# Two transformer blocks on one core: wide moving operands in both mixers, row-tiled index scores, a shorter bias and head

## The reference, cut to what matters

```python
h = rms_norm(x, norm_mix_g[l])
proj = h @ w_in[l]                       # q, k, v, xr, gr, sc_b, sc_c, sc_x, g_pre
...
s_own = s_own + rel_table[t5_bucket(dist)].transpose(2, 0, 1)      # the bias, by head
...
x = x + (g_a * y_a + g_b * y_b + g_c * y_c) @ w_out[l]
x = x + jnp.square(jax.nn.relu(rms_norm(x, norm_mlp_g[l]) @ w_mlp_up[l])) @ w_mlp_down[l]
x = rms_norm(x, final_g)
...
h = rmsnorm(x, g_mix) @ w_in             # z, xbc, dt, q, k, v, qi, ki, wi
s = jnp.einsum("bqhd,bsd->bqhs", qi_b, k_idx) * (IDX_HEAD_DIM ** -0.5)   # 16 index heads of 64
score = jnp.einsum("bqhs,bqh->bqs", jax.nn.relu(s), wi_b)
```

## Time and profile before

| | |
|---|---|
| median of three runs | 2725.01 us (2724.94 to 2727.85) |
| the profiled execution | 2726.56 us |
| its span | 2724.6 us |
| mean granted TensorE clock | 0.999 |
| PE busy | 2714.4 us (100%) |
| PE weight loads | 2360.8 us (87%) |
| DVE busy | 1668.2 us (61%) |
| ACT busy | 1279.5 us (47%) |
| L1676, L1677, L1678, the first mixer's units | 896 matmuls each |
| L1708, L1709, L1710, the second mixer's units | 592 matmuls each |
| L1691, L1692, the up projections | 2048 matmuls each |
| DMA | 509 MB, mean 187 GB/s |

### The profile page before, as it was taken

The page is one execution under the profiler, slowest core; times in us unless marked ns, Lnnn a source line. Parts: engine busy times, 40 slices in busy tenths (PEclk is TensorE's granted clock), DMA queues, the critical chain, the costliest instruction groups (busy, mean ns, idle before and its releaser), DMA issues.

```text
span 2724.6 us, 42567 instructions
## 1 busy us (share of the span) xinstructions
PE 2714.4 (100%) x15146; PEld 2360.8 (87%) x15146; DVE 1668.2 (61%) x2329; ACT 1279.5 (47%) x1721; POOL 23.2 (1%) x52
## 2 busy tenths in 40 slices
PE   9999999999999999999999999999999999999999
PEld 7999998888888888888888889999888888888887
DVE  5576766555555655655656566777776565565654
ACT  5455555444444544444434554455454344444443
POOL 0100000000000000000000000000000000000000
PEclk9999999999999999999999999999999999999999
DMA  7655555666665555555555555544455655555555
GB/s 276 199 171 176 181 174 185 201 198 197 204 210 188 180 190 193 185 193 189 189 193 185 186 185 163 171 149 155 154 178 187 195 190 186 192 186 193 189 188 170
DMA packets 140614, 509.01 MB, mean 187 GB/s; under 512 B 15975, under 2 KB 16231, under 8 KB 140232
## 3 DMA queue, kind: packets, MB, share of 16 engines
q1 hardware_dynamic: 135448, 492.28, 54.7%
q0 software_dynamic: 2736, 10.75, 1.2%
q10 hardware_dynamic: 2304, 4.20, 0.4%
HBM read 502.96 MB, written 4.19 MB: 186 GB/s over the span
## 4 chain that ended last, share of the span: by engine, by line
PE 98%; DVE 1%; ACT 1%; ACTq 0%; issue 0%
PE acc L1691 18%; PE acc L1692 9%; PE acc L1726 4%; PE acc L1728 4%; PE acc L1727 4%; PE pS L1726 4%; PE pT L1726 4%; PE pS L1727 4%; PE pS L1728 4%; PE pT L1728 4%; PE pT L1727 4%; PE acc L1676 4%; PE acc L1678 4%; PE acc L1677 4%; PE acc L1708 3%; PE acc L1710 3%
## 5 line engine op out<-in xcount | busy, mean ns | idle before, releaser
L989 DVE TENSOR_TENSOR wlo<-raw,whi 128x1024 fp32r<-128x1024 f32 x938 | 1147.6, 1224 | 845.5 <-ACT whi L530 843.5
L530 ACT ACTIVATE whi<-raw 128x1024 fp32r<-128x1024 f32 x938 | 992.4, 1059 | 1030.2 <-PE pT L1728 344.2
L1691 PE MATMUL acc<-a_w,whi 128*128 128x512 f32 x2048 | 724.6, 399 | 0.1
L1692 PE MATMUL acc<-a_w,wlo 128*128 128x256 f32 x2048 | 575.1, 281 | 0.0
L1691 PEld LDWEIGHTS acc<-a_w,whi 128*128 128x128 f32 x2048 | 384.8, 188 | 96.6 <-DVE a_w L1019 0.8
L1692 PEld LDWEIGHTS acc<-a_w,wlo 128*128 128x128 f32 x2048 | 386.9, 189 | 0.3
L1676 PE MATMUL acc<-a_w,whi 128*128 128x256 f32 x896 | 257.6, 287 | 0.0
L1678 PE MATMUL acc<-a_w,wlo 128*128 128x256 f32 x896 | 253.5, 283 | 0.0
L1677 PE MATMUL acc<-a_w,whi 128*128 128x256 f32 x896 | 253.5, 283 | 0.0
L1676 PEld LDWEIGHTS acc<-a_w,whi 128*128 128x128 f32 x896 | 171.8, 192 | 3.4 <-issue 3.0
L1708 PE MATMUL acc<-a_w,whi 128*128 128x256 f32 x592 | 173.9, 294 | 0.0
(11 more groups left out here) (406 smaller groups left out, 4215.7 us busy)
## 6 DMA issues: line engine op xcount, KB each, us to landing
raw<-stream SPq DMA_DIRECT2D x938, 512.0 KB, 3.3
gbias<-gateb POOLq DMA_DIRECT2D x12, 256.0 KB, 3.7
xF<-x ACTq DMA_DIRECT2D x8, 256.0 KB, 9.4
X<-x_rows POOLq DMA_DIRECT2D x1, 2048.0 KB, 9.0
bias_scratch<-brow POOLq DMA_DIRECT2D x8, 256.0 KB, 3.4
out<-X ACTq DMA_DIRECT2D x8, 256.0 KB, 4.6
bias<-bias_scratch POOLq DMA_DIRECT2D x8, 128.0 KB, 3.5
wg<-gates POOLq DMA_DIRECT2D x8, 128.0 KB, 3.4
```

The costliest lines, as they stand in the source:

```text
L530: A(whi[:, slot, :], raw[:, slot, :], ACT.Copy).then_inc(s.hi_done, 1)
L989: TT(wlo[:, slot, :], raw[:, slot, :], whi[:, slot, :].bitcast(F32), SUB).then_inc(s.lo_done, 1)
L1691: MM(ps, wh, wide[:, k0 + k, :], start=start and k == 0, stop=False, skip_group_check=True)
L1692: last = MM(ps[:, 0:T], wl, wide[:, k0 + k, 0:T], start=False, stop=not start and k == KC - 1, skip_group_check=True)
```

## The change

- First mixer: `chunk` goes; its units use `chunk_wide`. ACT copies the upper half of the bank to `half` (the renamed `sqacc`), DVE adds it to the lower half and then multiplies by `rB`.
- The last three steps of a head's attention (transposes, `attn_pt` and `attn_pv`, `attn_hi`, `attn_lo`) come one unit later, except for the last head.
- Second mixer: `half_unit` takes the same form. `unit_half` on ACT and `unit_sum` on DVE replace the copies from the bank; scaled units get a second DVE product (`unit_scaled`). The square of q reads `q_f` in SBUF and comes after the next `prep`. PE waits for `u_sum` alone.
- Index scores: 64 rows for each of the two heads, to two banks, instead of 128 rows against two diagonal blocks.
- Bias: one matmul with the table repeated 16 times for each head, one copy, eight DMAs that write the same rows.
- The first gates use the banks pV and pN instead of `acc`; the wait for the last evacuation moves to the first output product.
- Head: ACT issues two of the `xF` loads, SP the other six, two ahead of each of chunks 1 to 3.

```diff
@@ sync
             sp.dma_start(par, params).then_inc(s.par_landed, 16)
-            for c in range(NSLOT):
+            load(0, 0)
+            for c in range(1, NSLOT):
+                for k in (2 * c, 2 * c + 1):
+                    sp.dma_start(xF[:, 2 * k:2 * k + 2, :], x[:, 2 * k:2 * k + 2, :]).then_inc(x_landed[k], 16)
                 load(c, c)
@@ scalar
+                if j == (3 if t.base == 7 else 4):
+                    attn_pt(t)
                 if j == 3:
-                    attn_pt(t)
...
-                if j == 4:
+                if j == (4 if t.base == 7 else 5):
                     attn_hi(t, tile(br[0][0], t))
...
-            for k in range(8):
+            for k in range(2):
                 act.dma_start(xF[:, 2 * k:2 * k + 2, :], x[:, 2 * k:2 * k + 2, :]).then_inc(x_landed[k], 16)
...
                     prep(c)
+                    if i == 0 and j == 1:
+                        act.wait_ge(s.bias_ps, 1)
+                        A(brow, pO, ACT.Copy).then_inc(s.bias_copied, 1)
                     if i:
                         side1(j, At(i - 1))
+                    a = L1_UNITS * i + j
+                    act.wait_ge(s.mm_done, c.value(2))
+                    if a >= 2:
+                        act.wait_ge(s.l1_summed, a - 1)
+                    apart(act)
+                    A(half[:, a % 2, :], acc[a % 2][:, T:2 * T], ACT.Copy).then_inc(s.l1_copied, 1)
                     prep(c.plus(1))
...
+            def unit_half(u):
+
+                unit_done(unit_end(u))
+                if u == 0:
+                    act.wait_ge(s.t_evac, 2 * G_K + 2)
+                if u >= 2:
+                    act.wait_ge(s.u_sum, u - 1)
                 apart(act)
+                A(sq[:, u % 2, :], unit_bank(u)[:, T:2 * T], ACT.Copy).then_inc(s.u_half, 1)
...
                 attn_exp(At(8 + h))
+                unit_half(17 + 2 * h)
                 l2_prep(c + 1)
@@ vector
+            def evac(a, dst):
+
+                dve.wait_ge(s.l1_copied, a.value(1))
+                if a.least() > 0:
+                    dve.wait_ge(s.evacuated, a.value())
+                TT(t2, acc[a.mod(2)][:, 0:T], half[:, a.mod(2), :], ADD).then_inc(s.l1_summed, 1)
+                dve.wait_ge(s.l1_summed, a.value(1))
+                TT(dst, t2, rB, MUL).then_inc(s.evacuated, 1)
...
+            def unit_sum(u, dst):
+
+                dve.wait_ge(s.u_half, u + 1)
+                if u:
+                    dve.wait_ge(s.u_sum, u)
+                TT(dst, unit_bank(u)[:, 0:T], sq[:, u % 2, :], ADD).then_inc(s.u_sum, 1)
+
+            def unit_scaled(u, dst):
+
+                if u > 9:
+                    dve.wait_ge(s.evacuated, A_L2 + (u - 8) // 2 if u < 26 else A_L2 + u - 17)
+                unit_sum(u, usum)
+                dve.wait_ge(s.u_sum, u + 1)
+                TT(dst, usum, rB, MUL).then_inc(s.evacuated, 1)
@@ tensor
-                    MM(ps[:, 0:T], wh, hi, start=half == 0 and k == 0, stop=False)
-                    MM(ps[:, 0:T], wh, lo, start=False, stop=False)
-                    last = MM(ps[:, 0:T], wl, hi, start=False, stop=half == 1 and k == KC - 1)
+                    m = 8 * half + k
+                    MM(ps, wh, a_w[:, m, :], start=half == 0 and k == 0, stop=False, skip_group_check=True)
+                    last = MM(ps[:, 0:T], wl, a_w[:, m, 0:T], start=False, stop=half == 1 and k == KC - 1, skip_group_check=True)
...
-                if j == 2:
+                if j == (2 if t.base == 7 else 3):
                     attn_transpose(t)
...
-            def bias_rows(j):
-                for h in (2 * j, 2 * j + 1):
-                    if h >= 2:
-                        pe.wait_ge(s.bias_copied, h - 1)
-                    MM((pG if h % 2 else pO)[:, 0:512], tab[0:33, h:h + 1].to_broadcast([33, P]), oh[0:33, :],
-                       start=True, stop=True).then_inc(s.bias_ps, 1)
...
-                    chunk(c, a, a_w, 0, stop=False)
-                    chunk(c.plus(1), a, a_w, 8, start=False)
+                    chunk_wide(c, a, a_w, 0)
+                    chunk_wide(c.plus(1), a, a_w, 8, start=False)
...
-                    if i == 0 and j < 4:
-                        bias_rows(j)
+                        MM(pO, tab[0:33, :], oh[0:33, :], start=True, stop=True).then_inc(s.bias_ps, 1)
...
-                    banks = tbanks(i)
+                    banks = pair_first if side == 0 else tbanks(i)
...
-                q = qib[:, n % 3, :]
-                MM(pT[:, 0:T].rearrange("p (h k) -> p h k", h=2), q[:, 0:128],
-                   kibd.rearrange("p (h k) -> p h k", h=2)[:, :, 0:128], start=True, stop=True)
-                MM(pS[:, 0:2 * T], q[:, 128:256], kibd, start=True, stop=True).then_inc(s.idx_pe, 1)
+                rows = [slice(64 * e, 64 * e + 64) for e in range(2)]
+                for e, ps in enumerate((pT, pS)):
+                    r = rows[e]
+                    MM(ps[:, 0:128], qib[r, n % 3, 0:128], kibd[r, T * e:T * e + 128], start=True, stop=True)
+                for e, ps in enumerate((pT, pS)):
+                    r = rows[e]
+                    last = MM(ps[:, 128:384], qib[r, n % 3, 128:256], kibd[r, T * e:T * e + T], start=True, stop=True)
+                last.then_inc(s.idx_pe, 1)
```

More of the change, by code:

```diff
@@ L175, in __init__ @@
         self.up_copied = make("up_copied")
+        self.l1_copied = make("l1_copied")
+        self.l1_summed = make("l1_summed")
         self.setup_act = make("setup_act")
@@ L181, in __init__ @@
         self.bias_copied = make("bias_copied")
+        self.bias_out = make("bias_out")
         self.causal_landed = make("causal_landed")
@@ L208, in __init__ @@
         self.cleared = make("cleared")
-        self.unit_copied = make("unit_copied")
+        self.u_half = make("u_half")
+        self.u_sum = make("u_sum")
         self.k_sq = make("k_sq")
@@ L379, in program @@
         oh = take("oh", 512)
-        tab = take("tab", 8)
-        brow = take("brow", HEADS * 512).rearrange("p (k c) -> p k c", k=HEADS)
+        tab = take("tab", P)
+        brow = take("brow", 512)
         xF = take("xF", DT * T).rearrange("p (m t) -> p m t", t=T)
@@ L409, in program @@
         yst = take("yst", 8).rearrange("p (k h) -> p k h", h=2)
+        usum = take("usum", T)
         rg = take("rg", 8)[:, 0:4].rearrange("p (g h) -> p g h", h=2)
@@ L424, in program @@
         gb_landed = [ctx.enter_context(nc.semaphore(f"gb_landed{k}")) for k in range(2)]
-        bias_out = [ctx.enter_context(nc.semaphore(f"bias_out{k}")) for k in range(2)]
         def pcol(name, k=0):
@@ L860, in _ @@
             l2_prep(8)
-            unit_done(9)
-            apart(act)
-            A(sm_t, unit_bank(0)[:, 0:T], ACT.Copy).then_inc(s.unit_copied, 1)
+            unit_half(0)
             l2_prep(9)
@@ L948, in _ @@
                 ssd_exp(p)
+                unit_half(33 + p)
                 l2_prep(c + 1)
@@ L1202, in _ @@
                     else:
-                        evac(last, a, b.b)
+                        evac(a, b.b)
                     prep(c.plus(1))
@@ L1509, in _ @@
             V.tensor_copy(rB, pN[:, 0:T]).then_inc(s.rt_copied, 1)
+            unit_sum(0, sm_t)
             l2_prep(9)
@@ L1665, in _, with chunk_wide @@
             MM = nc.tensor.matmul
-            def chunk(c, a, wide, k0, start=True, stop=True):
+            def chunk_wide(c, a, wide, k0, start=True, late=None):
                 slot, ps = c.mod(NSLOT), acc[a.mod(2)]
@@ L1671, in chunk @@
                 if start and a.least() >= 2:
-                    pe.wait_ge(s.evacuated, a.value(-1))
-                for k in range(KC):
-                    wh, wl = (w[:, slot, P * k:P * k + P] for w in (whi, wlo))
-                    hi, lo = wide[:, k0 + k, 0:T], wide[:, k0 + k, T:2 * T]
-                    MM(ps[:, 0:T], wh, hi, start=start and k == 0, stop=False)
-                    MM(ps[:, 0:T], wh, lo, start=False, stop=False)
-                    last = MM(ps[:, 0:T], wl, hi, start=False, stop=stop and k == KC - 1)
-                last.then_inc(s.mm_done, 1)
-            def chunk_wide(c, a, wide, k0, start=True, late=None):
-                slot, ps = c.mod(NSLOT), acc[a.mod(2)]
-                pe.wait_ge(s.lo_done, c.value(1))
-                if start:
                     pe.wait_ge(s.evacuated, a.value(-1))
@@ L1698, in half_unit @@
                 if half == 0 and u >= 2:
-                    scaled = unit_scaled(u - 2)
-                    n = sum(unit_scaled(k) == scaled for k in range(u - 1))
-                    pe.wait_ge(s.evacuated if scaled else s.unit_copied, A_L2 + n if scaled else n)
+                    pe.wait_ge(s.u_sum, u - 1)
                 c, ps = At(B_L2 + c), unit_bank(u)
@@ L1843, in gates @@
                 def gates(c, i, side=None, turn=False):
-                    banks = tbanks(i)
+                    banks = pair_first if side == 0 else tbanks(i)
                     for j in range(8):
```

(11 more changed lines are left out.)

110 lines of the change are left out of this document (50 added, 60 removed).

## The result

The changed kernel takes 2705.09 us (median of four executions, 2703.81 to 2705.30), the kernel before 2724.98 beside it: ratio 0.9925, 95% interval 0.9911 to 0.9938. That is 19.9 us less at the median. The profiled executions are 2726.56 and 2704.91 us, their spans 2724.6 and 2702.9: 21.7 less, where the sum said 22.7. The range of the prediction (2696 to 2710) holds the time, and its centre, 2702.3, lies 2.8 us under the median. Of these 2.8, 1.8 come from the profiled executions that the sum compares: before's lay 1.5 us over its own median and after's 0.2 under. The other microsecond hides four errors of 0.4 to 1.4 us that nearly cancel.

What follows compares the result with a forecast made beforehand. PE was taken as the bound, busy 2714.4 of 2724.6 us. Gains of 9.7, 6.9, 2.3, 2.9, 1.1, 0.2 and 0.5 less 0.8 and 0.1 gave 22.7 us: 2702.3 us from the 2725.01 median, range 2696 to 2710.

Steps and rivals of the forecast that it cites:

- 512-column form: Both mixers' k-tiles: one matmul of 512 and one of 256 replace three of 256; 0.0065 us each, 9.7 us gained.
- bias: Bias head: one matmul on 33 rows and 512 columns replaces eight fp32 matmuls; 6.9 us gained, ends 6.5 to 7.1.
- index: Eight index steps: two row tiles of 64 save 0.29 us each, 2.3 us gained, ends 0 and 5.1.
- transposes: Attention: seven transposes one unit later find probabilities ready, 2.9 us gained; the eighth, in the gate stage, keeps its stop.
- bc: PE's wait for `bc` mostly goes, since ACT's square is queued behind the next `whi`; 0.2 us gained.
- head: Kernel's start: PE's first real matmul comes from 9.91 to about 9.4; 0.5 us gained.
- fifth round: Second mixer's fifth attention round: `attn_norm` queues behind the sum and product, so the probabilities come later; 0.8 us lost.
- sm_t: Second mixer's start: ACT's first half copy also waits for `kt` while PE turns `sm_t`; 0.1 us lost.
- No cost taken, save in two places: Units' longer ACT and DVE hand-over hides, except in the fifth attention round (-0.8) and at the second mixer's start (-0.1).
- 1.29 halves: Index steps' upper end: row tiles side by side halve the step exactly, 8 x 0.64, 5.1 us gained.
- Starved head: Rival at the kernel's start: stops of 2 us and a second half-clock stretch, 2706.0 us; chance 10%.
- A shorter idle may spare it: Kernel's start: a shorter PE idle may avoid the half clock of some 3 us, worth +1.7 us.

Runs made afterwards that it cites:

- split: Changed kernel, hand-over kept, with the 512-column matmul as two of 256 again in both mixers' units (each unit's first k-tile excepted): 2714.77 us.
- old_turn: Changed kernel with the transposes, attn_pt, attn_pv, attn_hi and attn_lo back in their units of before: 2710.55 us.
- old_head: Changed kernel with all eight loads of x issued by ACT and the four first chunks by SP, as before: 2703.07 us.
- x_small: Changed kernel with X loaded by four DMAs of 512 columns, issued together at the same place: 2702.28 us.
- kick_c: Changed kernel with the fifth k-tile's 256-column matmul as 128 + 128 in the six up groups that begin without an interruption: 2695.33 us.
- best2: Changed kernel with X in four DMAs, attn_norm first in the fifth round, q's sum before top-8, 128 + 128 in all eight up groups: 2688.85 us.
- kick: Changed kernel with one k-tile (once two) in another form in each of six up groups, six forms tried: 2702.92 us.
- idx_twice: Changed kernel with the four index matmuls of each of the eight steps issued twice, into the same banks: 2710.72 us (one execution).

## Why the prediction was right, and where it was not

| step of the sum | forecast | measured |
|---|---|---|
| 512-column form | 9.7 | about 11: some 5.9 in the first mixer, 5.2 in the second |
| bias | 6.9 | 7.2 (8.41 to 1.24 over the usual step) |
| index | 2.3 | 1.9 |
| transposes | 2.9 | 2.9: 3.3 for seven, less 0.5 at the eighth |
| gates on pV and pN | 1.1 | 1.1 |
| `bc` | 0.2 | 0.2 |
| head | +0.5 | -0.6 |
| fifth round | -0.8 | -1.0 |
| `sm_t` | -0.1 | -0.3 |
| first `q_stat` | none | -0.8 |
| sum, in spans | 22.7 | 21.7 |

- **Wide form.** Right in kind, and in the first mixer in size (6.6 ns a k-tile, 6.5 said). In the second mixer a k-tile gained 8.7 ns. The step that failed is that the sum takes the up loop's 0.3535 for both mixers: that is one of two rhythms, and 22 of the 51 stretches of the second mixer run in the other. split gives 9.7 for the 1395 k-tiles that it changes, which is 10.3 for 1488. The 11 is also what is left of the two stages when the other rows are taken off (11.1), and so it carries their errors.
- **Hand-over.** "No cost taken, save in two places" held for 93 units, but there was a third place. I checked where the new steps delay the bank and the probabilities, not who used to read the bank directly: the square of q did, and now stands behind DVE. The rule to have used was in the change's own list, where the square "reads `q_f` in SBUF and comes after the next `prep`"; I had counted that as a gain (`bc`) only. The `sm_t` term is 0.3 for the same reason.
- **Bias.** Within the bounds.
- **Index.** The 0.29 a step came from a neighbour, `ssd_y`; the step really gains 0.235. The column part is what full overlap gives, 0.64 of 1.29. The term that was not seen is the fixed 0.41, which the old step on the full array did not have and every step on a part of it has; it is why "1.29 halves" (5.1) did not happen. The neighbour carried most of it unseen: its 1.00 us holds 0.65 of columns. The Trainium skill (TensorE: Matmul & The Clock Gate, Part 3: Packing small matmuls) has row tiles run side by side, and the rows agree. It also has matmuls strictly in order, and the starts of the four matmuls are in the program's order here. What failed is the prediction's reading of that order, both passes of a tile ahead of the other tile's, which gave 0.6 us: the second pass of `pT` starts behind the first of `pS`, and the gain is 1.9.
- **Transposes.** Right, and by luck in part. The eighth, which I had said "keeps its stop", grew from 0.97 to 1.45 over the usual step. old_turn has it at 1.09, so 0.4 of that growth came with the steps that moved and only 0.1 with the new hand-over. I had priced a stop of 0.42 a head where 0.48 went; the two errors cancel (3.3 less 0.5). old_turn also shows that the other seven would have grown to 1.1 each if they had not moved.
- **Head.** The sign was wrong. The first real matmul came at 8.95, not 9.4, and no half clock fell in this execution: good for about 2.6 us (1.0, and 1.6 by old_head against before). Two stops of 1.57 and 1.30 took 2.9 (1.80 and 1.53 from start to start, 0.23 being usual); 0.3 more I did not find. The prediction had the mechanism, and priced it as a range of 0 to -2 at one chunk; it was the seventh chunk, and a second stop followed, since the late `wlo` pushed DVE's softplus chain (28.7 to 32.5) in front of the next but one. I took the middle, +0.5, where the row of `X`'s share (80.3%) and my own count of the chunks that were ahead of `X` ("some four" for eight) asked for the bad end; by the DMA issues, eight chunks had been issued ahead of it before and six now, of which three had landed when it was issued at 13.55. "Starved head" was a rival at 10%; its cause is what x_small shows. The Trainium skill (DMA: Bandwidth & Descriptors, Queues, rings and completion order) says that an engine takes its queues packet by packet, and both pairs of counts above agree.
- **Half clock.** "A shorter idle may spare it" fits, but is not the whole of it. PE's wait before the first real matmul, and the granted clock behind it: 2.0 us and 0.50 before; 1.4 and 1.00 in the changed kernel; 1.9 and 0.50 in kick_c; 3.2 and 1.00 in old_head; 2.9 and 1.00 in best2. Over all fourteen traces the clock fell to 0.50 behind waits of 1.9 to 2.1 us (five traces), and stayed at 1.00 behind the six shorter ones (1.3 to 1.8) and behind the three longer ones (2.2, 2.9 and 3.2). What decides is open. In the changed kernel it does not even cost: kick_c had it, and its first unit starts at 56.13 against 56.23, since the head then waits for weights anyway.

The range was right to reach 2710 and needlessly wide below. The forecast's error against the spans is 1.0 us; the four terms off by over 0.3 (+1.4, -0.4, -1.1, -0.8) would have allowed 3.7.

## What to carry to other kernels

On a saturated PE count matmuls as well as columns: 512 + 256 instead of 3 x 256 gave 7 to 9 ns on 360, and 1488 of them made half of this change. Small fp32 steps on a part of the array paid 0.35 to 0.41 us beside their columns here, and those on the full array nothing: row tiles gain only what they save in columns beyond that. When a reader of a bank is put behind another engine's evacuation, list every consumer of that result, not only the bank's next writer, and look what stands ahead of it in that engine's order. Look at the pieces of a bulk transfer beside a latency-bound stream: with pieces about as large as the stream's instead of four times as large, the first unit came 2.5 us earlier.

## What the runs showed of the hardware that was not expected

**Two rhythms of one instruction stream.** A stretch of wide k-tiles runs either at 353.3 ns (350, 361, 349, and again) or at about 346.7 (350, 343, 350, 344 in some stretches, 346, 347, 347 in others), and holds that until the next interruption. Two stretches of the changed kernel's second mixer, ten microseconds apart, same lines and same operands; 28 k-tiles in 9.88 us (0.3529), then 29 in 10.05 (0.3466):

```profile
1716.02 0.40 PE L1724 MATMUL acc<-a_w,whi 128*128 128x512 f32 x1
...
1725.90 0.40 PE L1724 MATMUL acc<-a_w,whi 128*128 128x512 f32 x1
...
1728.11 0.39 PE L1724 MATMUL acc<-a_w,whi 128*128 128x512 f32 x1
...
1738.16 0.40 PE L1724 MATMUL acc<-a_w,whi 128*128 128x512 f32 x1
```

Up groups that begin without an interruption, and have no k-tile in another form, were at 353.3 in every trace. The first group of each MLP, which the transposes of `turn_x` break, fell either way in kernels that are alike there (91.65 or 90.04 us in MLP 1, 91.73 or 90.13 in MLP 2). That is worth 1.6 us each. One program has one trace, so that the same program does both is not shown; but it fits the kernel before, whose executions stand near 2723.4, 2725.0 and 2726.5. The 128 + 128 form at the fifth k-tile sets the faster rhythm: fifteen groups of fifteen, one in kick, six in kick_c, eight in best2, the two first groups with it in their second unit among them. It makes two periods longer (404 and 401 ns in kick_c). The five other forms at the same place did not set it. That it is the length in nanoseconds that decides, and not the form, was argued and not shown, and why there are two rhythms is open. The narrow form shows only one in these traces, 360.

**A part of the array has a fixed price.** 0.41 us on 64 rows, 0.38 on 33 rows, 0.35 on 64 columns of the array, none on the full array (under idx_twice above).

**Queues share by packets**, not by bytes: 82 to 83 packets in four microseconds gave 1.34 MB to one and 0.34 MB to the other.
